# Two transformer blocks on one core: last two down units by column pairs, first unit of a stage by input chunks, inputs released by pairs, no stage fillers

## The reference

```
for l in range(2):                                  # first block
    x = x + 0.5 * swiglu(rmsnorm(x), ...)           # "ffn": 1024 -> 2 x 2816 -> 1024
    h = rmsnorm(x); z = h @ w_in                    # "mix1": conv, short conv, window attention,
    x = x + merged(z) @ w_out                       #   forgetting attention, gated and merged
    x = x + 0.5 * swiglu(rmsnorm(x), ...)           # "ffn"
for i in range(4):                                  # second block
    x = x + mixer[i](rmsnorm(x))                    # diff attention, hgrn, sgu, diff attention
    x = x + cross_attention(rmsnorm(x), mem_n)      # "cross"
    x = x + swiglu(rmsnorm(x), ...)                 # "ffn"
return rmsnorm(x)
```

## Time and profile before

| | us |
|---|---|
| median of 3 runs | 3505.65 |
| lowest, highest | 3504.89, 3505.94 |
| span of the profiled execution | 3503.2 |

### The profile page before, as it was taken

The page is one execution under the profiler, slowest core; times in us unless marked ns, Lnnn a source line. Parts: engine busy times, 40 slices in busy tenths (PEclk is TensorE's granted clock), DMA queues, the critical chain, the costliest instruction groups (busy, mean ns, idle before and its releaser), DMA issues.

```text
span 3503.2 us, 59063 instructions
## 1 busy us (share of the span) xinstructions
PE 3160.6 (90%) x24892; PEld 3070.7 (88%) x24892; DVE 1777.0 (51%) x1929; ACT 1293.2 (37%) x1295; POOL 2155.8 (62%) x464
## 2 busy tenths in 40 slices
PE   3996889999977899977999987999999999779998
PEld 3996779999976799976989987889999899769898
DVE  3639434736385347375347258526524373643472
ACT  2333434334333343333343453334343343334332
POOL 2884346887853468842748862357866488427485
PEclk7998889999997899987999999999999999879999
DMA  5553224554532244531425541234544345314252
GB/s 147 185 195 122 74 103 146 191 186 168 193 138 73 91 162 176 189 123 66 166 88 192 191 145 49 75 130 163 194 168 149 116 173 192 133 49 174 98 190 105
DMA packets 72966, 496.15 MB, mean 142 GB/s; under 512 B 7979, under 2 KB 12715, under 8 KB 13524
## 3 DMA queue, kind: packets, MB, share of 16 engines
q1 hardware_dynamic: 68884, 488.21, 39.5%
q10 hardware_dynamic: 3904, 5.26, 0.5%
HBM read 490.01 MB, written 3.41 MB: 141 GB/s over the span
## 4 chain that ended last, share of the span: by engine, by line
issue 56%; POOL 38%; PE 5%; POOLq 1%; DVE 0%; ACT 0%; DVEq 0%
POOL wl L365 38%; PE G L404 1%; PE G L405 1%; PE G L406 1%; PE S L405 1%; PE S L406 1%; PE S L404 1%; POOLq L369 0%; POOLq L364 0%; PE S L449 0%; DVE full L2101 0%; POOLq L365 0%; DVE root L1317 0%; DVE x L1463 0%; ACT full L930 0%
## 5 line engine op out<-in xcount | busy, mean ns | idle before, releaser
L365 POOL TENSOR_TENSOR wl<-raw,wh 128x2048 fp32r<-128x2048 f32 x460 | 2155.6, 4702 | 1315.3 <-ACT wh L908 1301.3
L404 PE MATMUL G<-ah,wl 128*128 128x256 f32 x4880 | 1404.3, 288 | 106.3 <-POOL wl L365 39.7
L405 PE MATMUL G<-al,wh 128*128 128x256 f32 x4880 | 1395.2, 286 | 0.0
L406 PE MATMUL G<-ah,wh 128*128 128x256 f32 x4880 | 1394.3, 286 | 0.0
L908 ACT ACTIVATE wh<-raw 128x2048 fp32r<-128x2048 f32 x457 | 866.8, 1910 | 774.4 <-PE G L406 393.3
L404 PEld LDWEIGHTS G<-ah,wl 128*128 128x128 f32 x4880 | 952.8, 195 | 117.2 <-issue 62.8
L405 PEld LDWEIGHTS G<-al,wh 128*128 128x128 f32 x4880 | 952.9, 195 | 0.2
L406 PEld LDWEIGHTS G<-ah,wh 128*128 128x128 f32 x4880 | 951.5, 195 | 0.0
L405 PE MATMUL S<-gl,wh 128*128 (+1 forms) x1408 | 398.5, 283 | 0.0
L406 PE MATMUL S<-gh,wh 128*128 (+1 forms) x1408 | 397.8, 282 | 0.0
L404 PE MATMUL S<-gh,wl 128*128 (+1 forms) x1408 | 394.6, 280 | 0.0
(11 more groups left out here) (301 smaller groups left out, 3725.7 us busy)
## 6 DMA issues: line engine op xcount, KB each, us to landing
raw<-w_units SPq DMA_DIRECT2D x460, 1024.0 KB, 4.8
bias<-tables ACTq DMA_DIRECT2D x24, 128.0 KB, 2.3
tables<-trow SPq DMA_DIRECT2D x1, 1536.0 KB
x<-x_in SPq DMA_DIRECT2D x1, 1024.0 KB, 4.7
con<-consts SPq DMA_DIRECT2D x1, 1024.0 KB, 14.8
memx<-mem_in ACTq DMA_DIRECT2D x1, 1024.0 KB, 5.7
out<-full SPq DMA_DIRECT2D x4, 256.0 KB, 2.5
tables<-trow SPq DMA_DIRECT2D x1, 768.0 KB
```

The source lines that it names most:

```text
L365: pool.tensor_tensor(wl[:, j * UW:(j + 1) * UW], raw[:, j * UW:(j + 1) * UW], wh[:, j * UW:(j + 1) * UW].bitcast(F32), ALU.subtract)\
L404: pe.matmul(out, sl, vh, start=start and k == 0, stop=False, **kw)
L405: pe.matmul(out, sh, vl, start=False, stop=False, **kw)
L406: ins = pe.matmul(out, sh, vh, start=False, stop=stop and k == len(parts) - 1, **kw)
```

## The change

1. The 14 matmuls of `WARM["stage"]` are gone in all stages.
2. `features_by_input` and `tokens_by_input`: the first unit of a stage that starts on `ah`, `al` goes over the input chunks in the outer loop and over both halves of the output in the inner one, and waits for `acts_ready` pair by pair, in token units too.
3. The last two down units of an ffn are done jointly: for each of four pairs of output chunks, first the unit before the last, then the last. After each of the first three pairs `columns_done` rises, and VectorE adds that pair to x. Both units' `unit_done` come in the fourth pair, the first one 12 matmuls before the end.
4. The last of the four output projections of diff, hgrn, sgu and cross goes by input chunks too and gives `inputs_free` after each of the first three pairs; ScalarE's `ah` of the next stage waits for that pair alone. After an ffn or mix1, ScalarE waits only for the units that read `ah`.
5. On ScalarE one weight copy (for the third unit of the next stage) is taken out of the ffn's end and put between the third and the fourth pair of `cut_input` (`deferred`).

```diff
-WARM = {"stage": 14, "level": 9, "head_norm": 12, "branch": 10, "first_level": 30, "gating": 24}
+WARM = {"level": 9, "head_norm": 12, "branch": 10, "first_level": 30, "gating": 24}
...
+            def features_by_input(out, j, xh, xl, acts=None, release=False):
+
+                for k in range(KD):
+                    if acts is not None and k % 2 == 0:
+                        pe.wait_ge(acts, c.next(acts))
+                    for fc in range(2):
+                        parts = [(wcut(wh, j, k * 256 + fc * P, P), wcut(wl, j, k * 256 + fc * P, P),
+                                  xh[:, k * T:(k + 1) * T], xl[:, k * T:(k + 1) * T])]
+                        ins = product(out[:, fc * 256:fc * 256 + T], parts, k == 0 and fc == 0, k == KD - 1,
+                                      skip_group_check=True)
+                    if release and k % 2 == 1 and k < KD - 1:
+                        ins.then_inc(inputs_free, 1)
+                return ins
...
-                keep_warm(WARM["stage"])
...
+                pe.wait_ge(gated_ready, r0 + FP)
+                pe.wait_ge(low_ready, n1 + FP)
+                for pair in range(KD // 2):
+                    for u in (FP - 2, FP - 1):
+                        j = (n1 + u) % RING
+                        for dc in (2 * pair, 2 * pair + 1):
+                            out = y[dc // 4][:, (dc % 4) * T:(dc % 4 + 1) * T]
+                            parts = [(wcut(wh, j, kt * D + dc * P, P), wcut(wl, j, kt * D + dc * P, P),
+                                      gh[:, u * 512 + kt * T:u * 512 + (kt + 1) * T],
+                                      gl[:, u * 512 + kt * T:u * 512 + (kt + 1) * T]) for kt in range(2)]
+                            ins = product(out, parts, False, u == FP - 1, skip_group_check=True)
+                        if pair == KD // 2 - 1:
+                            ins.then_inc(unit_done, 1)
+                    if pair < KD // 2 - 1:
+                        ins.then_inc(columns_done, 1)
...
-                projection(4, x_ready, ah, al, acts_ready)
+                projection(4, x_ready, ah, al, acts_ready, release=True)
...
             def cut_input(gain):
 
-                if unit[0]:
-                    act.wait_ge(unit_done, unit[0])
+                if inputs_read[0]:
+                    act.wait_ge(unit_done, inputs_read[0])
                 for k in range(KD // 2):
+                    if not inputs_read[0] and unit[0]:
+                        if k < KD // 2 - 1:
+                            act.wait_ge(inputs_free, c.next(inputs_free))
+                        else:
+                            act.wait_ge(unit_done, unit[0])
                     act.wait_ge(x_ready, c.next(x_ready))
...
                     ins.then_inc(acts_high, c.one(acts_high))
+                    if deferred[0] and k == KD // 2 - 2:
+                        deferred[0] = False
+                        n = unit[0] - 1 + LEAD
+                        high(n, n % RING, n // RING)
...
-                head, loops = segments(FP, 0)
+                head, loops = segments(FP - 1, 0)
                 step(head)
...
                 step(RING * last)
+                deferred[0] = unit[0] + LEAD < units
+                unit[0] += 1
...
-                dve.wait_ge(unit_done, unit[0])
                 y = [s_next(), s_next()]
                 for k in range(KD // 2):
+                    if k < KD // 2 - 1:
+                        dve.wait_ge(columns_done, c.next(columns_done))
+                    else:
+                        dve.wait_ge(unit_done, unit[0])
```

More of the change, by code:

```diff
@@ L271, in build @@
     gate_used = semaphore("gate_used")
+    columns_done = semaphore("columns_done")
+    inputs_free = semaphore("inputs_free")
     result = semaphore("result")
@@ L407, in product, with features @@
                 return ins
-            def features(out, j, xh, xl, acts=None, fcs=2, col=256):
+            def features(out, j, xh, xl, fcs=2, col=256):
                 for fc in range(fcs):
                     for k in range(KD):
-                        if acts is not None and fc == 0 and k % 2 == 0:
-                            pe.wait_ge(acts, c.next(acts))
                         parts = [(wcut(wh, j, k * 256 + fc * P, P), wcut(wl, j, k * 256 + fc * P, P),
@@ L417, in features, with tokens_by_input @@
                         ins = product(out[:, fc * col:fc * col + T], parts, k == 0, k == KD - 1)
+                return ins
[10 more added lines that the diff above has]
+                        ins.then_inc(inputs_free, 1)
+                return ins
+            def tokens_by_input(out, j, xh, xl, acts):
+                for k in range(KD):
+                    if k % 2 == 0:
+                        pe.wait_ge(acts, c.next(acts))
+                    for tb in range(TB):
+                        a = k * T + tb * P
+                        parts = [(xh[:, a:a + P], xl[:, a:a + P], wcut(wh, j, k * 256, 256), wcut(wl, j, k * 256, 256))]
+                        ins = product(out[:, tb * 256:(tb + 1) * 256], parts, k == 0 and tb == 0, k == KD - 1,
+                                      skip_group_check=True)
                 return ins
@@ L427, in tokens, with projection @@
                 return ins
-            def projection(count, by, xh, xl, acts=None, kind="features"):
+            def projection(count, by, xh, xl, acts=None, kind="features", release=False):
                 for u in range(count):
@@ L433, in projection @@
                     pe.wait_ge(low_ready, unit[0] + 1)
-                    if kind == "features":
-                        ins = features(out, j, xh, xl, acts if u == 0 else None)
-                    else:
-                        if acts is not None and u == 0:
-                            pe.wait_ge(acts, c.next(acts, KD // 2))
+                    first, freeing = acts if u == 0 else None, release and u == count - 1
+                    if kind == "features" and (first is not None or freeing):
+                        ins = features_by_input(out, j, xh, xl, first, freeing)
+                    elif kind == "features":
+                        ins = features(out, j, xh, xl)
+                    elif first is not None:
+                        ins = tokens_by_input(out, j, xh, xl, first)
+                    else:
                         ins = tokens(out, j, xh, xl)
@@ L491, in unit_of @@
                     pe.wait_ge(low_ready, n + 1)
-                    features(G[(g0 + j) % 4], (n0 + j) % RING, ah, al,
-                             acts_ready if u == 0 else None).then_inc(unit_done, 1)
+                    if u == 0:
+                        ins = features_by_input(G[g0 % 4], n0 % RING, ah, al, acts_ready)
+                    else:
+                        ins = features(G[(g0 + j) % 4], (n0 + j) % RING, ah, al)
+                    ins.then_inc(unit_done, 1)
                 head, loops = segments(2 * FP, 4)
@@ L892, in _ @@
             early = [0]
+            inputs_read = [0]
+            deferred = [False]
             gbank, sbank = [2], [0]
@@ L1031, in ffn @@
                 unit[0] += 2 * FP
+                inputs_read[0] = unit[0]
                 gbank[0] += 2 * FP
@@ L1176, in diff @@
                 cut()
+                inputs_read[0] = 0
                 passed(4)
```

7 lines of the change are left out of this document (3 added, 4 removed).

## The result

| | median us | lowest to highest | runs | ratio to before, 95% interval |
|---|---|---|---|---|
| before | 3505.27 | 3499.54 to 3505.94 | 4 | |
| changed | 3547.34 | 3546.47 to 3549.33 | 4 | 1.0123 [1.0109, 1.0138] |

The change makes the kernel slower by 42 us; 3539 was forecast, with 3512 to 3555 as range. The profiled execution's span went from 3503.2 to 3545.7 (+42.5).

The account below looks back on a forecast made before the run. The prediction took TensorE, busy for 90% of the span, as the bound. To 3505.65 it added 45.9 for held `al` and took off 8.2 at projections, 2.7 at cross stages, 1.5 at the end: 3539 us, range 3512 to 3555.

Parts of the forecast that it names:

- The deferred copy: At seven ffn ends GpSimd works from T+0.7 to T+10.2 and holds `al` twice: 45.9 us lost together.
- T: Moment when VectorE starts the addition to x released by the end of the last down unit or last projection.
- +7: At the seven ffn ends both GpSimd weight instructions come before the first `al`: 1.0 us more each.
- the 10 among the signs: Sign expected at the 7 ffn ends: the eight `al` take 10 us instead of 3.25.
- The clock after the hold: At ffn ends, after TensorE idles over 5 us, half clock loses 1.65 to 3.0 us each, middle 2.3.
- (a) and (b): Ffn ends before feature units (4 places, 32.5 us lost) and before token units (3 places, 13.4 lost).
- The projections: Six places, projection before an ffn: row sums at T+13.07 against T+14.44, 8.2 us saved, clock taken as 0.
- rival 4: At the six projections before an ffn the missing fillers also let the clock fall: +9, 3548 us; chance 10%.
- Cross and end: Four cross stages: earlier chain, 2.7 us saved; kernel's end: sums of squares run earlier, 1.5 us saved.
- GpSimd waiting for `al` (1): Rival at the ffn ends: GpSimd waits through all eight `al` and costs nothing, 3468 us; chance 12%.
- only one hold (2): Rival at the ffn ends: `al` slips through before GpSimd's second weight instruction, 3512 us; chance 8%.
- The clock staying up (3): Rival at the ffn ends: `al` is held twice but TensorE's clock doesn't fall, 3523 us; chance 8%.

Follow-up runs that it names:

- e_late: The changed kernel with the deferred weight copy moved behind the squares, next to the second copy: 3476.93 us, ratio 0.9928.
- e_pool_waits: The changed kernel with GpSimd waiting, at the seven ffn ends, until VectorE has added up the squares: 3477.45 us, ratio 0.9927.
- e_one_hold: The changed kernel with the second weight copy waiting until `al` is complete, the deferred copy left in place: 3521.81 us, ratio 1.0055.
- e_fill14: The changed kernel with the 14 fillers put back, nothing else: 3545.65 us, ratio 1.0123.
- e_joint_only: The kernel before with only the joint last two down units, their additions by `columns_done` and the deferred copy: 3562.22 us, ratio 1.0163.
- e_late_fill6: `e_late` with 6 fillers where the 14 were: 3461.24 us, ratio 0.9882.

## Why the prediction was right, and where it wasn't

*The deferred copy.* Right, in mechanism and nearly in size. GpSimd was forecast at T+0.70 and T+5.47; it started at T+0.64 and T+5.40. The stop-free run of TensorE was forecast from T+10.9 and began at T+10.97. `e_late`, `e_pool_waits` and `e_one_hold` show that this is the cause. One detail was wrong: I had the first `al` pass, since it would start 0.10 ahead. Its record does start 0.03 ahead of GpSimd's (259.53 against 259.56), and still it was the one held, for 4.84. At six of seven places the second one passed between GpSimd's two instead. There it cost nothing, since the first pair is ready at T+5.8 either way. At the third place none passed: the "+7" that I feared, which is 1.0 a place, came at one place. The eight `al` took 11.89, which is what my working gives; the 10 among the signs was a slip.

GpSimd was pushed back too, though I had called that not measurable: its second instruction took 4.82 or 4.83 at the six places where an `al` passed ahead of it, and 4.49 at the one where none did.

I had weighed a rule of the Trainium skill there (SBUF — State Buffer, "Who interferes with whom": who starts first keeps the shared pair, the other waits it out). On the waiting the trace agrees: each of the 14 held `al` at the seven places ends 0.28 or 0.29 after GpSimd's instruction. On who was first, the recorded starts don't fit as they stand, since the later record could win. But the lead decides. In the trace of the changed kernel, read to the nanosecond, VectorE's record was ahead by 27 to 33 ns in the eight meetings in which `al` was held, and by 36 to 48 ns in the six in which it passed. In `e_fill14` and `e_joint_only` those held were ahead by 23 to 34 ns, those that passed by 33 to 38. So the rule fits if about 34 ns are taken off VectorE's lead; that is an estimate from these leads, and no run varied the lead on purpose. It also says why I missed: I had the first `al` 0.10 ahead, and it was 0.03 ahead.

*The clock after the hold.* Mis-sized: 2.3 lost a place was forecast. At the first place the 84 matmuls from 269.89 to 281.56 took 11.67 in place of 10.08, so 1.6; over the seven places it was 0.1 to 2.1, 1.5 in the mean. With this (a) and (b) lost 41.5, not 45.9.

*The projections.* This step failed. I took 8.2 saved, and nothing for the clock; measured +0.7. TensorE started at T+1.7, where T+1.55 was forecast, and even the one place without a fall of the clock reached the row sums at T+13.3, not T+13.07: 1.5 us in all. At five of six places the clock fell a little after the start, and the units took 1.5 longer, 7.4 in all: my rival 4, which I gave 10%. The ffn behind the first mix1, from T on:

```profile
589.30:591.00 1.70, 0.00 (x0) 0.02 (x1) 1.70 (x4) 0.99 (x3) 0.89 (x1) 1.00 0.00 0
591.00:592.00 1.00, 0.99 (x8) 1.00 (x9) 1.00 (x4) 1.00 (x2) 0.00 (x0) 1.00 0.58 98
592.00:595.40 3.40, 3.40 (x18) 3.40 (x17) 3.33 (x7) 3.38 (x3) 0.71 (x1) 0.50 0.67 280
```

An idle of 1.7, a start at the full clock, and 1.0 later 3.4 us at 0.50. `e_late_fill6` shows it: 1.5 us of fillers give the 1.5 back.

*Cross and end.* -3.3 and -1.8, where -2.7 and -1.5 were forecast.

*The rest*, +5.4, had no step in the prediction. Two stretches hold more than all of it, the first diff stage and the third cross stage behind their row sums. Each pair is before, then after:

```profile
1509.70:1687.50 177.80, 134.91 (x916) 121.14 (x915) 98.24 (x166) 57.73 (x102) 67.86 (x15) 0.82 0.24 83
2679.70:2787.50 107.80, 100.21 (x792) 98.14 (x793) 35.81 (x51) 34.42 (x36) 68.19 (x15) 0.98 0.41 147
```

```profile
1538.30:1721.00 182.70, 137.73 (x916) 122.45 (x915) 100.11 (x166) 60.23 (x108) 67.81 (x15) 0.82 0.23 81
2720.20:2830.90 110.70, 103.07 (x792) 100.81 (x791) 30.84 (x52) 37.04 (x42) 67.94 (x15) 0.95 0.40 143
```

TensorE has the same number of records there. In the cross stage the mean clock fell from 0.98 to 0.95, which is the size of its 2.9 us. In the diff stage the mean over the stretch is the same, 0.82, but the half clock lies over other work. From a run of `S<-root,con` matmuls late in the stage (1656.22, now 1686.44) to the first `G<-ah,wl` behind it (1664.20, now 1697.51) the same work looks so, before and after:

```profile
1656.20:1664.20 8.00, 7.98 (x41) 7.21 (x41) 5.75 (x14) 4.32 (x5) 0.00 (x0) 0.79 0.00 1
```

```profile
1686.40:1697.50 11.10, 11.06 (x40) 9.41 (x41) 5.92 (x14) 4.32 (x5) 0.75 (x1) 0.56 0.01 2
```

This holds 3.1 of the 4.9 us, and the clock goes with it, 0.79 against 0.56. The other 1.8 weren't traced, and no run tested any of it.

So the sum came out 9 us low: 4.4 too much for the holds, 8.9 too little for the projections, 0.9 more gained at cross and end than forecast, 5.4 without a step. The errors go both ways, so part of the closeness of 3539 to 3547 is luck.

*The rivals.* GpSimd waiting for `al` (1) and only one hold (2) did not happen by themselves; `e_one_hold` made the second on purpose and gave 3522, where 3512 was worked out for it. Its row sums behind an ffn cost 19.2, where 19.0 was worked out; the 10 us lie at the projections, +2.2 in place of -8.2. The clock staying up (3) came near at one place of seven, where 0.1 was lost.

## What to carry to other kernels

When a chain behind a stage's end is shortened, ask what the other engines will now be doing beside it. Here the first kernel's low weights happened, at a stage's end, to be made before and after `al`, never beside it. The joint units free two weight slots together and late, and the place that the first of the two copies was given, between the third and the fourth `ah`, put GpSimd's instructions of 4.5 us onto VectorE's of 0.47 us that TensorE waits for. In a trace, look for the same instruction with two durations far apart (a median of 0.48 and a longest of 4.73): what ran beside the long one is the neighbour to keep away. And a part that loses alone can be the best part once its neighbour is moved: 1.0163 alone, 0.9819 with late copies and early `al`.

## What the runs showed of the hardware

- Two VectorE instructions with both operands in SBUF were held for 4.84 and 4.76 beside GpSimd's of 4.52 and 4.83, and ended 0.28 after them. At six of seven places one passed between, at the seventh none. Which of the two engines went first followed VectorE's lead in recorded start, in the changed kernel: up to 33 ns, held; from 36 ns on, passed.
- The additions to x, with one operand in PSUM, were never held: all 32 behind an ffn took 0.69, and 21 of them ran beside GpSimd.
- An idle of 1.7 us on TensorE was enough for the clock to fall to 0.50 shortly after, at five of six projections, with dense matmuls ahead and behind (busy for all of 570.0 to 589.1 at 1.00). The one that was spared is not a matter of the place: it is the fifth in the changed kernel, the fourth in `e_late`, and none in `e_one_hold`. The same idle at the seven ffn ends of `e_late` never did it. With 12 records of small fillers (1.5 us) in the idle the clock stayed at 1.00 at all thirteen places. What decides whether such an idle makes the clock fall is open.
